# Logits of the decay as rounded products over 96 rows in a hybrid GLA and short-convolution block

## The reference, cut to what matters

```python
n = rmsnorm(h, norm_w)
z = n @ w_in          # q 256, k 256, v 512, g 512, a_low 16, conv parts 4 x 512
log_a = log_sigmoid(a_low @ w_alpha_up + b_alpha) / 16      # a_low: 16 wide, out: 256 wide
# per chunk of 64 tokens: cum = cumsum(log_a); k_dec = k * exp(cum_end - cum)
#   state = exp(cum_end) * state + k_dec^T v ;  o = q^T state(end of chunk)
y_gla  = rmsnorm_per_head(o) * silu(g)
y_conv = cb * conv3(cc * cu) * silu(g_conv)
h = h + concat(y_gla, y_conv) @ w_out
h = h + sigmoid(h @ w_ple_gate + b) * (p @ w_ple);  out = rmsnorm(h)
```

## Time and profile before

| what | value |
|---|---|
| profiled execution | 2109.83 us |
| its span, first to last instruction | 2108.0 us |
| mean granted TensorE clock | 0.993 of 2.4 GHz |
| median of three runs | 2109.73 us |
| busy: TensorE, its weight loads | 96%, 79% |
| busy: VectorE, ScalarE, GpSimd | 65%, 35%, 28% |
| share of the ending chain: TensorE, VectorE | 87%, 9% |
| moved by DMA | 306.71 MB, mean 145 GB/s |

### The profile page before, as it was taken

The page is one execution under the profiler, slowest core; times in us unless marked ns, Lnnn a source line. Parts: engine busy times, 40 slices in busy tenths (PEclk is TensorE's granted clock), DMA queues, the critical chain, the costliest instruction groups (busy, mean ns, idle before and its releaser), DMA issues.

```text
span 2108.0 us, 25953 instructions
## 1 busy us (share of the span) xinstructions
PE 2032.0 (96%) x9762; PEld 1672.4 (79%) x9762; DVE 1375.2 (65%) x1537; ACT 732.0 (35%) x1062; POOL 596.9 (28%) x610
## 2 busy tenths in 40 slices
PE   4999999999999999999999999999999999999997
PEld 3887877778787788888888888888887888888885
DVE  7678877787775586756755765774565355555553
ACT  3444434344343443233323323323223233333331
POOL 7757667576655311111121121121111000000000
PEclk8999999999999999999999999999999999999999
DMA  5354453534545841223721125663376522222211
GB/s 216 120 198 157 160 190 130 204 144 164 194 154 190 336 167 36 95 78 144 262 85 56 60 85 214 210 229 131 120 249 229 190 90 90 89 74 74 83 74 46
DMA packets 82487, 306.71 MB, mean 145 GB/s; under 512 B 10192, under 2 KB 18784, under 8 KB 71904
## 3 DMA queue, kind: packets, MB, share of 16 engines
q1 hardware_dynamic: 53088, 179.14, 23.2%
q0 software_dynamic: 29312, 126.40, 16.6%
HBM read 183.87 MB, written 121.63 MB: 145 GB/s over the span
## 4 chain that ended last, share of the span: by engine, by line
PE 87%; DVE 9%; issue 2%; ACT 1%; DMA 1%; SPq 0%; DVEq 0%; ACTq 0%
PE bank L1007 14%; PE bank L1013 14%; PE bank L1009 14%; PE bank L764 12%; PE bank L772 12%; PE bank L765 12%; DVE XL L1453 2%; PE bank L1095 1%; PE bank L1094 1%; PE bank L1093 1%; DVE rt L1494 1%; PE bank L851 1%; PE bank L907 1%; PE bank L883 1%; DVE raw L1880 1%
## 5 line engine op out<-in xcount | busy, mean ns | idle before, releaser
L1007 PE MATMUL bank<-XH,WC 128*128 128x512 f32 x1344 | 525.3, 391 | 2.2 <-DVE xt L1784 2.0
L1013 PE MATMUL bank<-XL,WC 128*128 128x512 f32 x1344 | 523.6, 390 | 0.9 <-DVE XL L1618 0.9
L1009 PE MATMUL bank<-XH,WC 128*128 128x512 f32 x1344 | 523.7, 390 | 0.0
L1618 DVE TENSOR_TENSOR XL<-RQ,XH 128x1024 fp32r<-128x1024 f32 x168 | 205.8, 1260 | 236.9 <-ACT XH L1313 235.7
L1007 PEld LDWEIGHTS bank<-XH,WC 128*128 128x128 f32 x1344 | 252.6, 188 | 55.2 <-DVE xt L1784 2.5
L1013 PEld LDWEIGHTS bank<-XL,WC 128*128 128x128 f32 x1344 | 252.7, 188 | 54.0 <-DVE XL L1618 1.4
L1009 PEld LDWEIGHTS bank<-XH,WC 128*128 128x128 f32 x1344 | 252.7, 188 | 52.0
L709 POOL TENSOR_TENSOR RQ<-RQ 128x1024 f32<-128x1024 f32 x48 | 116.7, 2455 | 484.8 <-DVE RQ L1637 471.3
L1313 ACT ACTIVATE XH<-RQ 128x1024 fp32r<-128x1024 f32 x168 | 170.6, 1053 | 164.3 <-PE bank L1013 156.1
L765 PE MATMUL bank<-XH,WG 128*128 128x512 f32 x512 | 199.3, 389 | 0.0
L764 PE MATMUL bank<-XH,WG 128*128 128x512 f32 x512 | 199.3, 389 | 0.0
(11 more groups left out here) (184 smaller groups left out, 3512.9 us busy)
## 6 DMA issues: line engine op xcount, KB each, us to landing
WC<-w_scratch SPq DMA_DIRECT2D x21, 2048.0 KB, 8.7
RQ<-n_scratch POOLq DMA_DIRECT2D x32, 1024.0 KB, 5.4
w_scratch<-prep_hi POOLq DMA_DIRECT2D x84, 256.0 KB, 2.4
w_scratch<-PB POOLq DMA_DIRECT2D x84, 256.0 KB, 2.3
raw<-xb_dram SPq DMA_DIRECT2D x32, 512.0 KB, 6.4
n_scratch<-raw SPq DMA_DIRECT2D x8, 2048.0 KB, 6.4
y_scratch<-y_sb SPq DMA_DIRECT2D x64, 256.0 KB, 2.5
RQ<-y_scratch POOLq DMA_DIRECT2D x16, 1024.0 KB, 5.6
```

The lines of the kernel that those rows point to most:

```text
L1007: nc.tensor.matmul(bank[:], WC[:, i, q, 0, k], xh, start=(k == 0 and i in (P1, P2, P5)), stop=False, skip_group_check=True)
L1009: nc.tensor.matmul(bank[:], WC[:, i, q, 1, k], xh, start=False, stop=False, skip_group_check=True)
L1013: mm = nc.tensor.matmul(bank[:], WC[:, i, q, 0, k], xl, start=False, stop=(k == 3), skip_group_check=True)
L1618: nc.vector.tensor_tensor(XL[:, k], RQ[:, OPERAND[s % 7], 2 * h:2 * h + 2], XH[:, k].bitcast(F32), ALU.subtract).then_inc(sx_lo, 1)
```

## The change

The 16 channels of a_low are laid six times beside each other (`a_rep`, 96 columns for each token tile), transposed to 96 rows, and rounded. All 96 rows of `aT` then hold rounded values, six times the same 16; rows 32 to 47 are replaced by what the rounding left out (`a_low` on VectorE). `wup` gets 96 rows as well: the rounded weights in rows 0 to 15 and 32 to 47, what their rounding left out in rows 64 to 79, zeros elsewhere. One matmul on rounded operands over 96 rows so adds high x high, low x high and high x low. The diff, with what it touches in the order of the file:

```diff
+UP = 96
-        wup = over("wup", [RANK, QK], qg_at + 15 * BIG + QK * 4)
+        wup = over("wup", [UP, QK], qg_at + 15 * BIG + QK * 4, F32R)
-        aT = over("aT", [RANK, TB], at + 14 * ROW)
+        aT = over("aT", [UP, TB], at + 14 * ROW, F32R)
+        a_rep = over("a_rep", [P, TT, UP], at + 15 * ROW)
+        wup_raw = over("wup_raw", [UP, QK], sg_at + 6 * ROW)
...
-            sp.dma_start(wup[:], w_up).then_inc(consts_loaded, 16)
+            sp.wait_ge(memsets, 6)
+            for i in range(3):
+                sp.dma_start(wup_raw[32 * i:32 * i + RANK], w_up).then_inc(up_loaded, 16)
...
+            pool.memset(wup_raw[:], 0.0).then_inc(memsets, 1)
...
-                    mm = nc.tensor.transpose(ps[SMALL][0:RANK, t * P:t * P + P], ka_sb[:, t, QK:KA], ident[:])
+                    mm = nc.tensor.transpose(ps[SMALL][0:UP, t * P:t * P + P], a_rep[:, t], ident[:])
...
+                    pe.wait_ge(up_ready, 1)
...
             def ka_out(b, t):
                 if not is_first(b):
                     act.wait_ge(ds_done, NCH * b)
-                evacuate(b, ka_place(b, t), ka_sb[:, t], ps[MAIN[ka_place(b, t) % 3]][:, 0:KA])
+                    act.wait_ge(kdec, 2 * b)
+                wait_tile(act, GLA, b, ka_place(b, t))
+                bank = ps[MAIN[ka_place(b, t) % 3]]
+                nc.scalar.activation(ka_sb[:, t, 0:QK], bank[:, 0:QK], ACT.Copy)
+                nc.scalar.activation(a_rep[:, t].rearrange("p (i r) -> p i r", r=RANK),
+                                     bank[:, QK:KA].unsqueeze(1).broadcast_to([P, UP // RANK, RANK]),
+                                     ACT.Copy).then_inc(evacuated, 1)
...
-                nc.scalar.activation(aT[:], ps[SMALL][0:RANK, :], ACT.Copy).then_inc(aT_ready, 1)
+                nc.scalar.activation(aT[:], ps[SMALL][0:UP, :], ACT.Copy).then_inc(aT_hi, 1)
...
+            act.wait_ge(up_loaded, 48)
+            nc.scalar.activation(wup[:], wup_raw[:], ACT.Copy).then_inc(up_hi, 1)
...
+            def a_low(b):
+                dve.wait_ge(aT_hi, b + 1)
+                rows = slice(32, 32 + RANK)
+                nc.vector.tensor_tensor(aT[rows], ps[SMALL][rows, :], aT[rows].bitcast(F32),
+                                        ALU.subtract).then_inc(aT_ready, 1)
...
                 if nxt and tail:
-                    x_sums(b + 1, range(1, 4))
+                    x_sums(b + 1, range(1, 2))
+                if tail:
+                    a_low(b)
+                if nxt and tail:
+                    x_sums(b + 1, range(2, 4))
                 if tail:
                     split_squares(b - 1, 2)
+                if not tail:
+                    a_low(b)
                 add_bias(b, 0)
...
+            dve.wait_ge(up_hi, 1)
+            rows = slice(64, 64 + RANK)
+            nc.vector.tensor_tensor(wup[rows], wup_raw[rows], wup[rows].bitcast(F32), ALU.subtract).then_inc(up_ready, 1)
```

More of the change, by code:

```diff
@@ L227, in build @@
         aT_ready = sem("aT_ready")
+        aT_hi = sem("aT_hi")
+        up_loaded = sem("up_loaded")
+        up_hi = sem("up_hi")
+        up_ready = sem("up_ready")
         z_done = sem("z_done")
@@ L1121, in _ @@
             pe.wait_ge(memsets, 5)
-            pe.wait_ge(consts_loaded, 80)
+            pe.wait_ge(consts_loaded, 64)
             x_stats(0)
@@ L1428, in _ @@
             x_rms(0)
-            act.wait_ge(consts_loaded, 80)
+            act.wait_ge(consts_loaded, 64)
             nc.scalar.activation(suffix[:], mask[:, 0:P], ACT.Copy).then_inc(suffix_ready, 1)
@@ L1869, in _ @@
             x_sums(0, range(1, KT))
-            dve.wait_ge(consts_loaded, 80)
+            dve.wait_ge(consts_loaded, 64)
             dve.wait_ge(x_root, 1)
```

## The result

| | before | after |
|---|---|---|
| median (runs, lowest to highest) | 2113.43 us (14, 2108.19 to 2125.63) | 2125.93 us (14, 2117.14 to 2132.27) |
| ratio to before | | 1.0061, interval 1.0046 to 1.0077 |
| profiled execution, span | 2109.83, 2108.0 | 2126.12, 2124.3 |
| GpSimd's last stores issued | 699.47 | 724.02 |
| SP issues the first conv weights | 704.28 | 728.10 |

The prediction was 2103.5, faster. The kernel became slower by 0.6%. The rows of the table from the profiled execution down are of one execution of each kernel; a second one of each is read in experiment 1. Part 4 of the page after, the shares of the ending chain, already says where to look: before it was TensorE 87% and VectorE 9%, now GpSimd and its DMAs stand on it.

The account below looks back on a forecast made before the run. TensorE, busy 96% of the span, was taken to bound the kernel, with late conv weights binding at the border. Against 2109.83, -7.7 - 0.9 + 2.3 = -6.3 gave 2103.5 us, range 2096 to 2110.

Parts of the forecast that it names:

- Logits: GLA stage, TensorE: each of 16 logits calls shortens by 1.0 us, 16 us in all, ends 9.6 and 20.
- the prediction's two readings: Logits' tiling mode on TensorE: 96 rows run as 128, giving 16 us, or are one more mode, giving 9.6.
- Transposes, ScalarE, the start: GLA blocks and kernel start: wider transposes, split ScalarE copies and added setup work were all taken to cost 0.
- The low part on VectorE: Each GLA block: one added VectorE operation of 0.69 us, finished before TensorE wants aT, so costing TensorE nothing.
- VectorE just follows: GLA tail blocks: VectorE's idle shrinks to 0.3 us; 0.2 lost per block, 1.2 to 1.5 us in all.
- GpSimd's last stores don't move: End of GpSimd's weight splitting beside the GLA stage: stores stay at 699.47, so SP issues at 704.3 as before.
- The border: GLA to conv stage: weights land at 718.2, so 7.7 of 14.8 us arrive and 7.1 become a DMA wait.
- half clock behind it: Conv stage start: after TensorE's idle the granted clock falls to half pace, taken as 2.3 us lost.
- the XL wait: Early conv stage: TensorE's 0.93 us wait at 729.30 for a VectorE operation falls away, -0.9 us.
- rival (c): Border: the weights come late and the kernel is slower, 2113.5 us at 10 us of store delay; chance 0.07.
- its own rule: Border, late last store: 8.2 us slack used first, no longer faster from about 6 us delay, 2113.5 at 10.

Follow-up runs that it names:

- experiment 1: Both kernels run again unedited: the kernel before 2111.85 us (ratio 0.9997), the changed kernel 2127.01 us (1.0056).
- experiment 7: Both kernels with GpSimd's whole preparation beside the GLA stage replaced by HBM-to-HBM copies of the same sizes: before 2077.82 us, after 2060.99.
- experiment 4: Changed kernel without VectorE's new operation a_low, the low part missing from the logits: 2123.63 us, ratio 1.0029.
- experiment 3: Changed kernel with each logits matmul issued five times, so a call takes 1.28 us, as before the change: 2116.85 us, ratio 0.9988.
- experiment 8: Kernels of experiment 7 with the pairs' arithmetic put back on constants: before 2086.76 us, after 2073.38; after with the pairs' DMAs instead, no arithmetic: 2061.90.
- experiment 6: Both kernels with GpSimd loading each gate-stage tile before splitting the previous one: before 2107.55 us (0.9959), after 2109.13 us (0.9965).

## Why the prediction was wrong, step by step

*Logits*, 16 x 1.0 = 16 us: right. Two calls in the profile cost 0.32 and 0.23, and experiment 7 gives 16.8 in all. The gaps of 0.35 and 0.33 us in the weight loads around the 16-row group are gone with 96 rows, as by the first of the prediction's two readings of the Trainium skill, "TensorEngine Tiling (Array Packing)", Key Properties. That page speaks of a drain at a change of tiling mode and lists no row tile of 96; that 96 rows run as 128 is how the trace reads here.

*Transposes, ScalarE, the start*, 0: nothing speaks against it. ScalarE's copy of 96 rows took 0.59, as that of 16. By the two calls above the logits are worth 14.9 to 16.3, and the kernels of experiment 7 differ by 16.8, which leaves no room for a cost of these.

*The low part on VectorE*, 0.69, hidden: its size is right (0.68 in the timeline), and by experiment 4 the blocks stay long without it.

*VectorE just follows*, 1.2 to 1.5 lost in all: wrong in size in the first pair of profiles, where TensorE's waits for VectorE rose by 10 us and brought another 4 of half clock, and not in the second, where they fell by 1.5 and the loss was the same. So this is not what made the sign. I had seen the cause and left it there: "one of them lasts longer than 0.69, up to 1.8; I put that down to GpSimd working on the same memory". The durations that I put into the sum were those of one meeting of the two engines in the old order. In the shorter block they meet elsewhere: the sums' mean went from 1.01 to 1.52 us, that of XL from 1.22 to 0.89, and the total stayed.

*"GpSimd's last stores don't move"*: this is the step that failed and that made the sign. They moved from 699.47 to 724.02, and in the second pair from 703.72 to 717.32. I took GpSimd's own pace as a property of GpSimd; yet each of its pairs ends and begins with transfers that share the DMA engines with SP's, and SP's go with the blocks. 24 of the 24.6 us are longer waits for these two transfers. That it is this meeting, and not something else in those queues, rests on the timelines and is not shown: no experiment moved SP's transfers alone, and experiment 3 had a last store at 721.07 with the long logits.

*The border*: right in its form, a DMA as releaser, half clock behind it (2.9 against 2.3), the XL wait gone. With the weights 23 us late in place of 0.5, the wait is 17.6 and not 7.1. It is the prediction's rival (c), held at 0.07 and priced at 2113.5 for a store 10 us late; what spoke for it was called "nothing but the shared port, and VectorE's slowed sums". It had the right path but not the cause that is found here, which is the very thing it set against itself, GpSimd's DMA round trips. By its own rule (+3.7 us at 10, one more for each further microsecond) 24.6 gives +18.3, and 16.3 came. The issue stood 4.1 us behind the last stores in place of 4.8, and the landing took 12.6 in place of 13.4. The chance was too low because I asked what could make GpSimd slower, and not whether its place in the block was worth anything.

**What stays open.** Splitting the pairs costs 34.6 us in the kernel after (2095.56 against 2060.99) and 24.3 in the kernel before (2102.15 against 2077.82), and the arithmetic of experiment 8 explains 12.4 and 8.9. The rest I put down to the free-running order, where long blocks of 91 us stand beside pairs of 45: a block and two pairs keep step and meet at the same operations again and again. That is how I read the four long blocks; no run forced the phase to show it. Nor is it known why the kernel before gained from experiment 6.

## What to carry to other kernels

An engine that runs "beside" a stage is only at its own pace as long as nothing it shares changes; before a sum says that its last event doesn't move, look at what each of its waits shares with the stage that is about to become shorter. When a stage is shortened, the slack of everything joined at its end shrinks by the same amount, so price the latest joiner late by the slack and more, not only on time. And where a VectorE operation lasts longer than its like in the trace, find its partner on GpSimd first: that surplus is a matter of order and need not stay where it is.

## What the runs showed of the hardware

- VectorE with two operands in SBUF against GpSimd's arithmetic: 0.69 us alone, up to 2.30 for one of 512 columns; with an operand in PSUM 0.69 throughout. The edit left the total of the four groups as it was (123.6 and 123.3 us) and moved it from one to another.
- GpSimd's DMAs by themselves, 12 pairs of 2 loads and 14 stores of 256 to 512 KB, in place of copies of the same sizes, cost the blocks nothing that can be seen (80.7 us in both, 0.9 us in all).
- The scatter from execution to execution, 9 to 28 us in ten and more runs of each kernel that splits its weights, is about 3 us or less in four or five runs of those without GpSimd's arithmetic or with it paced by the blocks. So it goes with the free-running arithmetic; that it is made by the order of the two engines is my reading.
- 2 MB of weights took 13.4 and 12.6 us at the border with six more pieces issued behind them, and 11.4 alone; in the last case the DMA engines' share was 1.00 meanwhile (416 GB/s from 708 to 720 us), with the other queues' transfers.
